# Two hybrid blocks on one core: the value products of all 64-column heads turned round, two heads side by side in the array

## What is computed

```python
# block one, per layer
h = rmsnorm(x, norm_mix[l]);  proj = h @ w_in[l]          # 3476 columns
y_m = mlstm(...)      # 4 heads of 128 columns
y_b = moba(...)       # 4 heads of 64 columns, causal softmax
y_n = nsa(...)        # 4 heads of 64: gate0 * compressed + gate1 * selected + gate2 * window
x = x + concat(y_m, y_b, y_n) @ w_out[l]
h = rmsnorm(x, norm_ffn[l]);  x = x + square(relu(h @ w_ff1[l])) @ w_ff2[l]
...
# block two, per layer
p = rms_norm(x, g_pre) @ w_in_2[l]                        # 12 x 512 columns and 8
ya = diff_attention(...) * silu(ga)                       # 4 heads of 128 columns
yb = stick_breaking_attention(...) * silu(gs)             # 8 heads of 64
yc = forgetting_attention(...) * silu(gf)                 # 8 heads of 64
x = x + rms_norm(concat(ya, yb, yc) @ w_out_2[l], g_post)
```

## Time and profile before

| | |
|---|---|
| median of 3 runs | 1093.7 us (1092.07 to 1094.06) |
| profiled execution: its time | 1093.48 us |
| profiled execution: span of its instructions | 1091.7 us |
| TensorE busy | 1070.7 us, 98% |
| VectorE busy | 737.6 us, 68% |
| ScalarE busy | 619.4 us, 57% |
| GpSimd busy | 62.0 us, 6% |
| granted TensorE clock | 1.0 |

### The profile page before, as it was taken

The page is one execution under the profiler, slowest core; times in us unless marked ns, Lnnn a source line. Parts: engine busy times, 40 slices in busy tenths (PEclk is TensorE's granted clock), DMA queues, the critical chain, the costliest instruction groups (busy, mean ns, idle before and its releaser), DMA issues.

```text
span 1091.7 us, 16525 instructions
## 1 busy us (share of the span) xinstructions
PE 1070.7 (98%) x6300; PEld 913.0 (84%) x6300; DVE 737.6 (68%) x1280; ACT 619.4 (57%) x1039; POOL 62.0 (6%) x80
## 2 busy tenths in 40 slices
PE   9999999999999999999999999999999999999997
PEld 7888878888888988888888887898988778989886
DVE  5789777677667888687766675773455756844555
ACT  6776754344436768563444354857556558565562
POOL 1010110000000100110000000004000000040000
PEclk9999999999999999999999999999999999999999
DMA  9853365555657544346566644654444456544441
GB/s 314 270 154 117 97 190 180 190 173 186 210 183 215 169 114 133 123 152 200 170 213 193 193 156 137 211 155 136 118 135 137 132 155 195 154 137 134 136 134 59
DMA packets 89403, 179.03 MB, mean 164 GB/s; under 512 B 8989, under 2 KB 20637, under 8 KB 89325
## 3 DMA queue, kind: packets, MB, share of 16 engines
q1 hardware_dynamic: 88605, 176.58, 52.0%
q10 hardware_dynamic: 720, 1.40, 0.4%
HBM read 176.90 MB, written 1.05 MB: 163 GB/s over the span
## 4 chain that ended last, share of the span: by engine, by line
PE 83%; DVE 7%; ACT 4%; issue 3%; DMA 1%; SPq 1%; DVEq 0%; POOL 0%; POOLq 0%; ACTq 0%
PE bank L830 19%; PE bank L832 18%; PE bank L831 18%; PE bank L896 11%; PE bank L898 5%; DVE w_lo L1767 2%; PE bank L982 2%; PE bank L931 2%; PE bank L1029 1%; ACT w_hi L1368 1%; DMA raw<-in_w_in 1%; PE bank L1039 1%; PE bank L1038 1%; PE bank L1037 1%; PE bank L1292 1%
## 5 line engine op out<-in xcount | busy, mean ns | idle before, releaser
L1767 DVE TENSOR_TENSOR w_lo<-raw,w_hi 128x1024 fp32r<-128x1024 f32 (+1 forms) x319 | 385.4, 1220 | 238.1 <-ACT w_hi L1368 235.3
L1368 ACT ACTIVATE w_hi<-raw 128x1024 fp32r<-128x1024 f32 (+1 forms) x319 | 331.0, 1054 | 182.8 <-PE bank L832 96.6
L830 PE MATMUL bank<-w_hi,h_parts 128*128 128x512 f32 (+1 forms) x448 | 179.9, 402 | 2.9 <-DVE w_lo L1809 1.5
L896 PE MATMUL bank<-h_parts,w_hi 128*128 128x512 f32 x512 | 181.5, 398 | 1.0 <-DVE arena L2131 0.7
L832 PE MATMUL bank<-w_hi,h_parts 128*128 128x512 f32 (+1 forms) x448 | 173.5, 387 | 0.0
L831 PE MATMUL bank<-w_lo,h_parts 128*128 128x512 f32 (+1 forms) x448 | 173.3, 387 | 0.0
L898 PE MATMUL bank<-h_parts,w_lo 128*128 128x256 f32 x512 | 143.6, 280 | 0.0
L896 PEld LDWEIGHTS bank<-h_parts,w_hi 128*128 128x128 f32 x512 | 96.1, 188 | 25.5 <-issue 2.6
L830 PE MATMUL bank<-h_parts,w_hi 128*128 128x256 f32 x384 | 112.3, 292 | 1.0 <-DVE w_lo L1767 1.0
L832 PE MATMUL bank<-h_parts,w_lo 128*128 128x256 f32 x384 | 108.5, 282 | 0.0
L831 PE MATMUL bank<-h_parts,w_hi 128*128 128x256 f32 x384 | 108.5, 282 | 0.0
(11 more groups left out here) (294 smaller groups left out, 1542.7 us busy)
## 6 DMA issues: line engine op xcount, KB each, us to landing
raw<-in_w_in SPq DMA_DIRECT2D x143, 512.0 KB, 3.9
raw<-in_w_ff SPq DMA_DIRECT2D x128, 512.0 KB, 4.3
raw<-in_w_out SPq DMA_DIRECT2D x40, 512.0 KB, 3.3
raw<-in_w_in SPq DMA_DIRECT2D x8, 404.0 KB, 5.4
xn<-in_cmp_w SPq DMA_DIRECT2D x8, 256.0 KB, 5.3
x_sb<-in_x SPq DMA_DIRECT2D x2, 512.0 KB, 9.2
mix<-in_cmp_w SPq DMA_DIRECT2D x4, 256.0 KB, 4.2
gain<-in_cmp_w SPq DMA_DIRECT2D x4, 256.0 KB, 5.6
```

The source lines that it names most:

```text
L830: pe.matmul(out_ap, s_hi, m_hi, start=start, stop=False, **kw)
L896: pe.matmul(ps[:, :].rearrange("p (a t) -> p a t", a=2), hi[:, kk, f], h_parts[:, :, k, :], start=k == 0, stop=False, skip_group_check=True)
L1368: act.activation(slot(w_hi, u), slot(raw, u), ACT.Copy).then_inc(hi_ready, 1)
L1767: dve.tensor_tensor(slot(w_lo, u), slot(raw, u), slot(w_hi, u).bitcast(F32), ALU.subtract)\
```

## The change

All heads with 64 columns (12 in block one, 8 stick-breaking and 8 forgetting heads in block two) make their value products with the values stationary and the turned weights moving, two heads at once on the two halves of the array's columns (`value_pair`). The output comes by feature, so that the tiles of `mix` for these heads are no longer turned.

Row sums can't be divided out behind such a product (tokens are on the free axis), so a new stage N, at the step of E, does it ahead of the transposes: VectorE computes the inverses of a pair (`row_inverses`), GpSimd multiplies `probs` with them (`scale_weights`), and T waits for GpSimd. Selected, window and compressed branch add up in one bank. The stages V now go by pairs, at the odd head's step. In block two the gates 7 and 11 become feature units; VectorE evacuates them, ScalarE takes the silu at p = 33 and 48 (`gate_silu`), and the product with the gate is three steps: `mix_full` (VectorE), `mix_hi` (ScalarE), `mix_lo` (VectorE).

```diff
-FEATURE2 = (4, 5, 8, 9)
+FEATURE2 = (4, 5, 7, 8, 9, 11)
+BY_FEATURE = ("att1", "fox",)
...
+    def columns_of(kind, h):
+        if kind == "att1" and h > 3:
+            return 1, 4, 11
+        return h // 4, h - h % 4, h - h % 4 + 3
...
-            for stage, lag in (("V", 4), ("T", 2), ("E", 1), ("S", 0)):
-                for h in range(12):
+            for stage, lag in (("V", 4), ("T", 2), ("E", 1), ("N", 1), ("S", 0)):
+                for h in range(stage == "V", 12, 2 if stage in ("V", "N") else 1):
...
-                if p == 25:
-                    single(2, "mix_turn", 0, l, 2)
...
-                    single(3, "cmp_o", l)
+                    step("cmp_o", l)
...
-                single(7, "mix_turn", 0, l, 3)
...
-        LAGS = {... "fox": (("V", 3), ("T", 2), ("E", 1), ("S", 0))}
+        LAGS = {... "fox": (("V", 3), ("T", 2), ("E", 1), ("N", 1), ("S", 0))}
...
-                for h in range(8):
-                    late = h % 2 if stage == "V" else 0
-                    if 26 + 3 * (h // 2) + lag + late == p:
+                for h in range(stage == "V", 8, 2 if stage == "V" else 1):
+                    if 26 + 3 * (h // 2) + lag == p:
...
-            if p == 46: ... single(i, "mix_turn", 1, l, 1, i)
-            if p == 54: ... single(4 + i, "mix_turn", 1, l, 2, i)
+            if p in (33, 48):
+                step("gate_silu", l, p // 48)
+            for n, full_at in enumerate((34, 38, 49, 52)):
+                for c, part_of in enumerate(("mix_full", "mix_hi", "mix_lo")):
+                    if p == full_at + c:
+                        step(part_of, l, n)
...
+            def value_pair(ps, lo, values_of, weights_of, first):
+                for b in range(NT):
+                    for c in range(2):
+                        mm = pe.matmul(ps[HD * c:HD * c + HD, lo + b * P:lo + T], values_of[c](b), weights_of[c][:, b * T:T + b * P],
+                                       start=first and b == 0, stop=b == 1, skip_group_check=True)
+                return mm
...
+                    elif kind in BY_FEATURE:
+                        pe.wait_ge(weights_scaled[kind], len(heads_of(kind, l)) * l + h + 1)
                     else:
                         pe.wait_ge(exp_ready, nth_head(kind, l, h))
...
+                        if s[2] == "V" and s[3] in (3, 11):          # ScalarE
+                            g = s[3] // 8
+                            turned(("att1", l, "O", g), mixT1_hi[1][:, 2 * g:2 * g + 2, :])
...
+                    elif kind == "gate_silu":
+                        n = s[2]
+                        for i in range(NT):
+                            drained(act, ("proj", 1, l, 7 + 4 * n, i))
+                            act.activation(gateT[:, n, 2 * i:2 * i + 2, :], gateT[:, n, 2 * i:2 * i + 2, :], ACT.Silu).then_inc(gate_ready, 1)
+                        act.preload_act_table_set(LOG_EXP)
...
+            def scale_weights(kind, l, h):
+                pool.wait_ge(inverse_ready[kind], len(heads_of(kind, l)) // 2 * l + h // 2 + 1)
+                for c in range(2):
+                    blocks_of = probs[:, (h + c) % 3, :].rearrange("p (b t) -> p b t", b=3)
+                    pool.tensor_tensor(blocks_of, blocks_of, block_inv[:, h // 2 % 2, c, :].unsqueeze(2).broadcast_to([P, 3, P]),
+                                       ALU.mult).then_inc(weights_scaled[kind], 1)
...
+            def row_inverses(kind, l, h, gate):
+                dve.wait_ge(exp_ready, nth_head(kind, l, h + 1))
+                g, r = divmod(h, 4)
+                dst, inv, sums = block_inv[:, h // 2 % 2], row_inv[:, 0:2, :], row_sum[:, g % 2, r:r + 2, :]
+                if gate is None:
+                    link(dve.reciprocal(dst[:, :, 0:2], sums))
+                    dve.reciprocal(dst[:, :, 2:3], sums[:, :, 1:2]).then_inc(inverse_ready[kind], 1)
+                else:
+                    link(dve.reciprocal(inv, sums))
+                    tt(dst[:, :, 0:2], inv, gate, ALU.mult)
+                    dve.tensor_tensor(dst[:, :, 2:3], inv[:, :, 1:2], gate[:, :, 1:2], ALU.mult).then_inc(inverse_ready[kind], 1)
...
-                def epilogue1(g):
...
-                def gated(name, p, g, weights):
...
+                    elif kind == "mix_full":
+                        dve.wait_ge(gate_ready, 4 * l + 2 * (n // 2) + n % 2 + 1)
+                        free(dve.tensor_tensor(mixed(n), ps[:, :].rearrange("p (c t) -> p c t", c=2),
+                                               gateT[:, n // 2, 2 * (n % 2):2 * (n % 2) + 2, :], ALU.mult), key)
```

More of the change, by code:

```diff
@@ L191, in head_steps @@
             use((*name, "T", h), 6)
+        elif stage == "V" and name[0] in BY_FEATURE:
+            g, first, last = columns_of(name[0], h)
+            if h == first + 1:
+                use((*name, "O", g), 7)
+            if h == last:
+                done((*name, "O", g))
         elif stage == "V" and name[0] == "diff":
@@ L405, in side2 @@
                 for stage, lag in LAGS[name[0]]:
-                    for h in range(0, 8, 2 if name[0] == "diff" and stage in ("V", "T", "C") else 1):
+                    by_pair = ("V", "T", "C") if name[0] == "diff" else ("V", "N")
+                    for h in range(name[0] == "fox" and stage == "V", 8, 2 if stage in by_pair else 1):
                         lead = h - h % 2 if stage in ("E", "S") else h
@@ L562, in hybrid_blocks @@
         row_nb = few(4, NT)
+        block_inv = few(2, 2, 3)
         row_sum, row_inv = few(2, 4, NT), few(4, NT)
@@ L597, in hybrid_blocks @@
         values = part(0, 3, NT, 512)
-        gates = part(3072, NT, 3, 512)
+        gates = part(3072, NT, 512)
+        gateT = part(4096, 2, 4, T)
         featT = part(6144, 16, T)
@@ L1030, in head_stage @@
                     close(mm, (*name, "T", h))
+                elif kind in BY_FEATURE:
+                    g, first, last = columns_of(kind, h)
+                    for c in range(2):
+                        drained(pe, (*name, "T", h - 1 + c))
+                    ps = open_bank((*name, "O", g)) if h == first + 1 else bank[bank_of[(*name, "O", g)]]
+                    mm = value_pair(ps, h // 2 % 2 * T, [heads_of(kind, l)[h - 1 + c][3] for c in range(2)],
+                                    [probsT[:, (h - 1 + c) % 3, :] for c in range(2)], h == first + 1)
+                    if h == last:
+                        close(mm, (*name, "O", g))
                 else:
@@ L1217, in _ @@
                         pair = s[3]
[L1218 to L1223 removed]
+                        pe.wait_ge(mlstm_mixed, 2 * l + pair + 1)
                         turn(s, mix, [(2 * pair + c, i) for c in range(2) for i in range(NT)])
@@ L1605, in _ @@
                             else:
-                                free(act.activation(gates[:, i, j // 4, :], ps[:, :], ACT.Silu, scale=r), key)
-                        if j % 4 == 3:
+                                free(act.activation(gates[:, i, :], ps[:, :], ACT.Silu, scale=r), key)
+                        if j == 3:
                             act.preload_act_table_set(LOG_EXP)
+                    elif kind == "gate_silu":
[4 more added lines that the diff above has]
+                        act.preload_act_table_set(LOG_EXP)
+                    elif kind == "mix_hi":
+                        n = s[2]
+                        drained(act, ("fox" if n > 1 else "stick", l, "O", n % 2))
+                        act.activation(mixT_hi[1 + n // 2][:, 2 * (n % 2):2 * (n % 2) + 2, :], mixed(n), ACT.Copy).then_inc(mixed_hi, 1)
                     elif kind == "turn2":
@@ L1718, in _ @@
                         row_rstd(s[1])
+                    elif kind == "fox" and s[2] == "N":
+                        scale_weights("fox", l, s[3])
                     elif s == ("diff", l, "V", 6):
@@ L2092, in _ @@
                             free(dve.tensor_copy(probsT[:, s[3] % 3, :], ps[:, 0:384]), s)
-                        elif s[2] == "V" and s[3] % 4 == 3:
-                            epilogue1(s[3] // 4)
+                        elif s[2] == "N":
+                            g, r = divmod(s[3], 4)
+                            gate = n_gate[:, :, s[3]:s[3] + 2].rearrange("p i h -> p h i") if g else None
+                            row_inverses("att1", l, s[3], gate)
+                        elif s[2] == "V" and s[3] in (3, 11):
+                            g = s[3] // 8
+                            turned(("att1", l, "O", g), mixT1_hi[1][:, 2 * g:2 * g + 2, :], mixT1_lo[1][:, 2 * g:2 * g + 2, :])
                     elif kind == "mlstm_end" and s[3] == 0:
@@ L2259, in _ @@
                         free(dve.scalar_tensor_tensor(softp[:, h % 2, :], ps[:, 0:384], 0.0, softp[:, h % 2, :], ALU.max, ALU.add), z)
-                    elif kind == "stick" and s[2] == "V" and s[3] % 4 == 3:
-                        gated(("stick", l, "O", s[3] // 4), 1, s[3] // 4, None)
                     elif kind == "mix_turn":
```

135 lines of the change are left out of this document (51 added, 84 removed).

## The result

The changed kernel takes **1116.34 us** (median of four runs, 1114.67 to 1118.28), the kernel before 1093.85 in the runs beside it: the ratio is 1.021, with a 95% interval from 1.0195 to 1.0225. It is 22.5 us slower. I had forecast slower, by 7.6. The profiled execution took 1114.67, the shortest of the four, and its span is 1112.7.

A forecast was written before the change was run, and what follows sets the result against it. TensorE, busy 98% of the span, was taken as the bound, with VectorE almost a second one in block one's attention. 1093.5 + 13.2 (block one) - 5.4 (block two) = 1101.3 us, range 1090 to 1109.

The forecast's parts named there:

- The turned tiles' waits are replaced by waits two units later, which I take as free: Block two: waits for turned tiles move two units later and add no time.
- the mixing in three small steps: Block two: the gate product's small steps lie beside products; were that cover gone, 0.7 us each.
- at head 6 (+1.8): Block two, fourth forget pair: the moved silu stands ahead of its exponentials, making them 1.8 us late per layer.
- -5.4: Block two's total over both layers, in us, from -2.7 per layer.
- 13.2: Block one's attention: added time over both layers in us, from +6.6 per layer.
- 3.0, 5.5, 6.4 and 7.85 late: Block one, second to fifth pairs: lateness in us of the transposes, adding up because VectorE waits for TensorE in between.
- my rival of 1090.0: Block one: waits don't add up because VectorE's place stays, 0.95 us remains per layer; total 1090.0 us, chance 0.13.
- What I gave TensorE back after head 8 (0.9 and 0.35): Block one, after the fifth pair: TensorE wins back two turns, 0.9 us, and 0.35 on values.
- the sixth pair: Block one's last pair of heads: claimed covered, with no wait of its own charged.
- 0.9 for a value pair: TensorE: the new value pair takes 0.9 us, against 1.22 for a pair of heads before.
- forecast 5.6: Block one: TensorE alone saves 2.8 us per layer, 5.6 over both.
- I charged 1.0 us per pair: Block one: GpSimd and VectorE block each other, one of a pair's two scalings charged at 1.0 us, ends 0 and 2.0.

The follow-up runs named there:

- Run 1: Changed kernel plus TensorE products on a constant tile filling its waits in block one and at block two's bank 7: 1107.18 us, ratio 1.0131.
- run 6: Block one as before the change, block two as changed, with VectorE multiplying the first forget group by its gates one unit earlier: 1088.7 us.
- run 7: Block one as before, block two as changed, with the first forget group's gate product and ScalarE's last gate silu each one unit earlier: 1086.55 us.
- runs 9 and 4: Changed kernel, block one unscaled: 9 computes inverses on VectorE that nothing awaits, 1091.41 us; 4 also has GpSimd multiply constants aside, 1100.82 us.

## Why the prediction was wrong, step by step

The forecast was 1101.3 us with a range to 1109, measured 1116.3. Sign and mechanism were right, three sizes were not. The 15.0 us split into about 9.2, 3.5 and 2.4. The first is a difference of medians, the others are shifts of single traces, so the split is good to 2 us or so: by the traces alone it is 7.3, 3.5 and 2.4, and the changed kernel's median lies 1.7 above its profiled execution.

**The clock, 9.2 us, unpriced.** I had named a fall of the granted clock as a way to be wrong and put no time on it. Run 1 measures it: with the clock up in block one the time is 1107.2, inside my range. This is the step that failed most: a forecast with waits of 3 us in front of TensorE ought to have carried a term for it.

**Block two, 3.5 us.** "The turned tiles' waits are replaced by waits two units later, which I take as free" is the step that failed. They weren't free, and neither was what I wrote beside it, that "the mixing in three small steps" lies beside products: the first of these steps frees bank 7, and TensorE waits 1.96 us per layer for it, with a stretch at half clock behind it in the first layer. I had looked for the wait one step further on, at head 6 (+1.8), where run 6 then shows it (1.36) once the bank is free. The sum of the savings was too large as well. I forecast -5.4 with 1.8 of wait per layer in it, so -9.0 without; run 7, with both steps in their better places and 0.53 of wait per layer, gives -6.1, so about -7.1 without. Of the 1.9 that are missing, about 1.3 are two small waits in each layer that the kernel before doesn't have there, 0.23 and 0.59 us, less 0.15 by which another got shorter. These are rows of run 7:

```profile
775.88 0.87 PE L1039 MATMUL bank<-probs,arena 128*64 128x256 f32 x8 [0.23 <-DVE mix L2311]
...
784.33 0.70 PE L1334 MATMUL bank<-vecs,const 128*128 128x256 f32 x2 [0.59 <-DVE vecs L2324]
```

**Block one without the clock, 2.4 us** (15.6 less 13.2). Run 1 is the kernel to compare here; it stood 0.5 later at head 0 than the changed one. Forecast for heads 2, 4, 6 and 8: 3.0, 5.5, 6.4 and 7.85 late. Run 1 shows 3.9, 6.0, 6.9 and 8.6, less the 0.5: each within 0.5 of the forecast. That the places add up, against my rival of 1090.0, is shown. That each comes so close is in part luck, since GpSimd's product is shorter than I took it there and VectorE is held up at more places than I had charged (below). What I gave TensorE back after head 8 (0.9 and 0.35) is not there: run 1's first feed-forward product is 8.3 late in the first layer and 7.3 later again in the second, where I had 6.6 each. This is where the 2.4 come from. Here the sixth pair, which I had called covered, waits 0.90 in the changed kernel.

**TensorE's own saving.** 0.9 for a value pair was 0.80. Without N block one gains 4.3 us over both layers by the landmark (forecast 5.6), so the value pairs and turns together are right to 1.3 us.

**The chain of N.** A pair's inverses with the step to GpSimd take 0.45 us (71.15 to 71.60), as I took them (0.43). GpSimd's product is 0.83 where nothing holds it, near my lower end of 0.8, and 1.02 on average in 52 to 118 (I had taken 1.0).

**The collision of GpSimd and VectorE.** I charged 1.0 us per pair from two rows. VectorE's own loss is 9.0 us for 12 pairs by its busy time in runs 9 and 4, so 0.75 per pair (the taps are 0.5 of it). It cost about as much as it was long: 9.4 us for both layers with TensorE waiting for none of GpSimd's products, because VectorE had no slack and is itself waited for. I had put this loss in front of the fourth and fifth pair only; it comes at every pair. Of GpSimd's 2.60 us for two products it is the second that is held up; TensorE goes on at 72.48, at the end of the first, so at head 2 this is not in the chain. The Trainium skill, page "SBUF — State Buffer", section "SBUF: two separate sides", lets the one that starts first have the shared ports for its whole instruction; that fits GpSimd's 2.60 us for two products beside a `w_lo`, and that `w_lo` itself hardly grew (1221 to 1243 ns).

By runs, then, and added up from the kernel without N: inverses on VectorE 4.1 us (1087.3 to 1091.4), GpSimd's products beside them 9.4 (to 1100.8), TensorE's waits for both 6.4 (to 1107.2), the clock 9.2 (to 1116.3). By the landmark of the second layer's feed-forward, which leaves block two out, the same four are 5.6, 9.1, 5.3 and 7.3. Runs 9 and 4 have falls of the clock of their own and run 1 has none here, so some of the clock's cost is in the second term and missing in the third. The order of the steps is mine, and another order could share them out differently.

## What to carry to other kernels

Here a factor applied to an output was off the path; the same factor applied to an input stood in front of the engine that sets the time. Before moving it, ask which engine's stream it will stand in, how full that engine is there, and which step stands right behind it: here the change pays in the block where VectorE is busy 27.8 of 52 us and costs in the one where it is busy 54.7 of 60. When a forecast has new waits of 2 or 3 us on TensorE, give the clock a term of its own. And when a step moves, look at what frees the bank, not only at what fills it.

## What the runs showed of the hardware that I had not expected

In the changed kernel TensorE's granted clock fell to 0.50 (1.2 GHz) six times, each time within or right behind a wait of 1.8 to 3.2 us, and stayed there for 3.4 or 6.8 us; the first wait, 3.04 us at head 2, brought no fall, and the same wait in the second layer (3.03 us, to 401.97) did. So the length of a wait alone did not tell here whether the clock would fall. With products on a constant tile in the same waits it stayed at 1.00 in both attention stretches, and the kernel was 9.2 us faster for it. And GpSimd's products cost time without TensorE needing them: 24 of 128x384, 0.83 us each where nothing held them up, kept VectorE busy 9.0 us longer and made the kernel 9.4 us longer.
